# Down projection of a decoder step: the last norm in two token halves, the first of them inside the second pass

## What is computed

```python
def rmsnorm(x, g):
    xf = x.astype(jnp.float32)
    y = xf * lax.rsqrt(jnp.mean(xf * xf, axis=-1, keepdims=True) + EPS)
    return (y * g.astype(jnp.float32)).astype(x.dtype)
...
    f = (jax.nn.silu(h @ w_ff_gate) * (h @ w_ff_up)) @ w_ff_down
    x = x + ga2 * rmsnorm(f, g_post_ffn)
```

## Time and profile before

| | us |
|---|---|
| median of 3 runs | 2390.45 (2389.07 to 2390.79) |
| span of the profiled execution | 2391.5 |
| TensorE busy in the span | 2167.8 (91%) |
| VectorE, ScalarE, GpSimd busy | 880.6, 434.5, 501.2 |
| `stage_ffn_down`, first to last product | 276.1 |
| from the last product to the end | 49.8 |

### The profile page before, as it was taken

How to read it: one execution, slowest core, us unless ns; L and a number is a source line. 1 busy time by engine, 2 the same in 40 slices (tenths; PEclk the granted TensorE clock), 3 DMA queues, 4 the chain that set the end, 5 groups by cost and what they waited for, 6 DMA issues and landing times. The chain is left out here.

```text
span 2391.5 us, 31036 instructions
## 1 busy us (share of the span) xinstructions
PE 2167.8 (91%) x11898; PEld 1749.6 (73%) x11898; DVE 880.6 (37%) x1519; ACT 434.5 (18%) x896; POOL 501.2 (21%) x453
## 2 busy tenths in 40 slices
PE   3789999897778888999999998799999999999994
PEld 3678888676445565788888664688888888888883
DVE  1444122662345665522121116522222222534336
ACT  0241000331234555110000012311111000000001
POOL 2112210012211111521211113622223222001002
PEclk9899999895789999999999999899999999999997
DMA  9432112654410000111211210311111111122421
GB/s 240 120 95 75 44 36 57 184 130 132 116 49 1 2 1 1 36 45 27 53 26 44 90 51 3 108 35 53 35 52 36 36 53 35 49 97 84 152 79 73
DMA packets 238588, 157.35 MB, mean 66 GB/s; under 512 B 34502, under 2 KB 230632, under 8 KB 238417
## 3 DMA queue, kind: packets, MB, share of 16 engines
q1 hardware_dynamic: 224734, 138.33, 20.5%
q0 software_dynamic: 3600, 14.78, 1.8%
q10 hardware_dynamic: 10146, 2.80, 0.6%
HBM read 143.33 MB, written 16.71 MB: 67 GB/s over the span
## 5 line engine op out<-in xcount | busy, mean ns | idle before, releaser
L210 PE MATMUL ps<-hT,ring 128*128 128x264 f32 x2144 | 495.9, 389 | 18.7 <-DVEq L3025 14.8
L210 PE MATMUL ps<-big,ring 128*128 128x264 f32 (+1 forms) x2080 | 503.2, 400 | 4.5 <-DVEq L2863 4.5
L210 PEld LDWEIGHTS ps<-hT,ring 128*128 128x128 f32 x2144 | 410.2, 192 | 91.4 <-DVEq L3025 14.9
L210 PEld LDWEIGHTS ps<-big,ring 128*128 128x128 f32 x2080 | 396.0, 190 | 101.3 <-DVEq L2863 4.9
L3230 PE MATMUL ps<-big,ring 128*128 128x264 f32 x1056 | 240.7, 388 | 2.9 <-PEq L3417 2.9
L3230 PEld LDWEIGHTS ps<-big,ring 128*128 128x128 f32 x1056 | 201.7, 191 | 38.1 <-issue 3.2
L210 PE MATMUL ps<-big 128*128 128x264 f32 x608 | 138.5, 386 | 0.0
L210 PEld LDWEIGHTS ps<-big 128*128 128x128 f32 x608 | 115.4, 190 | 20.1 <-issue 0.4
L2610 DVE TENSOR_TENSOR big<-big,ps 128x528 f32<-128x528 f32 x70 | 49.3, 704 | 184.7 <-PE ps L210 177.2
L3080 POOL TENSOR_TENSOR ring<-ring 128x512 f32<-128x512 f32 x22 | 30.0, 1365 | 366.1 <-DMA ring<-in_w_ff_up 363.9
L975 DVE TENSOR_TENSOR big<-big,ps 128x528 f32<-128x528 f32 x63 | 44.2, 703 | 163.7 <-PE ps L210 163.3
(11 more groups left out here) (454 smaller groups left out, 2596.7 us busy)
## 6 DMA issues: line engine op xcount, KB each, us to landing
ring<-in_w_ada SPq DMA_DIRECT2D x44, 512.0 KB, 5.5
ring<-in_w_in SPq DMA_DIRECT2D x34, 512.0 KB, 5.1
ring<-in_w_ff_down SPq DMA_DIRECT2D x16, 1024.0 KB, 4.9
ring<-in_w_ff_gate SPq DMA_DIRECT2D x22, 512.0 KB, 4.0
ring<-in_w_ff_up SPq DMA_DIRECT2D x22, 512.0 KB, 5.2
ring<-in_w_ff_down SPq DMA_DIRECT2D x8, 768.0 KB, 4.2
x_kept<-big SPq DMA_DIRECT2D x8, 528.0 KB, 7.5
big<-x_kept SPq DMA_DIRECT2D x16, 264.0 KB, 6.2
```

The costliest lines, as they stand in the source:

```text
L210: ins = pe.matmul(out, w[:, k, :], rhs(k), start=first and k == 0, stop=last and k == nk - 1)
```

## The change

Line 3037 of `stage_ffn_up` writes the hidden values in token order, so pass 0 of the down projection holds tokens 0 to 527 whole and pass 1 tokens 528 to 1055. The rest is in `stage_ffn_down`:

- `tile`, the squares and the additions to `acc` work on whole token halves.
- At the start of steps 13 and 16 (c = 1 of pairs 4 and 5) TensorE sums 264 columns of the first half's `acc` into the free bank; at the end of these steps' queue of sums VectorE adds EPS and takes the reciprocal (`inverse`). Behind pair 4's squares ScalarE waits for both and takes one root. GpSimd then multiplies all eight tiles of the first half, ahead of adding the squares of pair 5. VectorE's eight `residual` steps stand two each behind the weight sums in steps 18, 19, 21 and 22.
- The squares of the last pair are no longer added by GpSimd: TensorE sums `acc` and the two squares into one bank for each 264 columns.
- ScalarE takes the two last roots between the copies of row tiles 1 and 2, and 2 and 3. Both must be done before the second half is scaled.
- The row tiles are twelve of 88 tokens: tiles 0 to 5 need the first half alone, 6 to 11 all of the second, sample tokens included. Three PSUM buffers of two banks and six row buffers serve them. The last tile is stored as 56 rows of `y_p` and 32 of `y_s`.

```diff
-                        f = to[:, bass.ds(it * 2 + hh, 1), :].rearrange("p o (n h t) -> p (o h) n t", h=2, n=2)
+                        f = to[:, bass.ds(it * 2 + hh, 1), :].rearrange("p o (h n t) -> p (o h) n t", h=2, n=2)
...
+YT = 88
+YN = T // YT
...
     def tile(s, unit, h):
-        return m.hT[:, unit, HALF * h + NH * s:HALF * h + NH * (s + 1)]
+        return m.hT[:, unit, HALF * s + NH * h:HALF * s + NH * (h + 1)]
...
         @block.gpsimd
-            for t in range(2 * N_SUM):
-                n = t // 2
-                a = both(m.acc[:, :], n // (N_SUM // 2))
+            for t in range(LATE):
+                if t == KD + 2:
+                    pool.wait_ge(rt_ok, 1)
+                    for k in range(KD):
+                        f = m.hT[:, k, 0:HALF]
+                        pool.tensor_tensor(f, f, rst[0], ALU.mult).then_inc(scaled, 1)
+                a = m.acc[:, halves[t // KD]]
...
         @block.tensor
+                if c == 1 and FIRST <= n < FIRST + 2:
+                    x = n - FIRST
+                    pe.wait_ge(pre, 1)
+                    pe.wait_ge(acc_ok, 1 + KD)
+                    pe.wait_ge(joined, 7 * (n - 1) + 6)
+                    pe.matmul(ps[:, bank(n, 7), 0:NH], ones, m.acc[:, NH * x:NH * (x + 1)], start=True,
+                              stop=True).then_inc(ss_mm, 1)
...
+                if c == 0 and FIRST < n <= FIRST + 2:
+                    pe.wait_ge(ss_out, n - FIRST)
...
+            pe.wait_ge(acc_ok, 1 + LATE)
+            pe.wait_ge(joined, 7 * (N_SUM - 2) + 6)
+            pe.wait_ge(copied, N_SUM)
+            for x in range(2):
+                pe.matmul(ps[:, x, 0:NH], ones, m.acc[:, HALF + NH * x:HALF + NH * (x + 1)], start=True, stop=False)
+            for t in range(2):
+                pe.wait_ge(sq_ok, LATE + t + 1)
+                for x in range(2):
+                    ins = pe.matmul(ps[:, x, 0:NH], ones, sq[t][:, NH * x:NH * (x + 1)], start=False, stop=t == 1)
...
         @block.scalar
+                if n == FIRST:
+                    act.wait_ge(r_ok, 2)
+                    act.activation(rst[0], rst[0], ACT.Sqrt).then_inc(rt_ok, 1)
+            for i in range(YN):
+                if i in (2, 3):
+                    x = i - 2
+                    r = rst[1][:, NH * x:NH * (x + 1)]
+                    act.wait_ge(r_ok, 3 + x)
+                    act.activation(r, r, ACT.Sqrt).then_inc(rt_ok, 1)
...
         @block.vector
+                if c == 1 and FIRST <= n < FIRST + 2:
+                    x = n - FIRST
+                    inverse(x, bank(n, 7), rst[0][:, NH * x:NH * (x + 1)])
+                if c < 2 and n >= FIRST + 2:
+                    if n == FIRST + 2 and c == 0:
+                        dve.wait_ge(x2_in, 16 * 2 * KD)
+                    for k in range(2):
+                        residual(4 * (n - FIRST - 2) + 2 * c + k)
```

More of the change, by code:

```diff
@@ L3146, in stage_ffn_down @@
             (m.ring[:, 2, 0:4, :], m.ring[:, 2, 4:8, :], block4(spare[:, 512:1024]))]
-    sq = [spare[:, 1024 + HALF * i:1024 + HALF * (i + 1)].rearrange("p (h t) -> p h t", h=2) for i in range(2)]
+    sq = [spare[:, 1024 + HALF * i:1024 + HALF * (i + 1)] for i in range(2)]
     ones = m.rest[:, 9 * NH:9 * NH + P]
-    rst = m.products[:, 0:T]
-    rows = [m.products[:, T + D * i:T + D * (i + 1)] for i in range(4)]
+    rst = [m.fore[:, KD + s, 0:HALF] for s in range(2)]
+    NR = 6
+    rows = [m.products[:, D * i:D * (i + 1)] for i in range(NR)]
     steps = [Down(m, i, sums[i % 2]) for i in range(len(STEPS))]
@@ L3195, in _ @@
                             sp.dma_start(x2(k, h), m.x2_kept[:, k, halves[h]]).then_inc(x2_in, 16)
-            for i in range(TT):
+            for i in range(YN):
                 rows_ready(sp, i)
[L3198 to L3203, removed]
+                n = min(YT, SEQ - YT * i)
+                sp.dma_start(O["y_p"][0, YT * i:YT * i + n, :], rows[i % NR][0:n, :]).then_inc(stored[i % NR], 16)
+                if n < YT:
+                    sp.dma_start(O["y_s"].rearrange("b s d -> (b s) d"), rows[i % NR][n:YT, :]).then_inc(
+                        stored[i % NR], 16)
+            for i in range(NR):
+                sp.wait_ge(stored[i], 16 * (len(range(i, YN, NR)) + (i == (YN - 1) % NR)))
         @block.gpsimd
@@ L3214, in _ @@
                 pool.tensor_tensor(a, a, sq[t % 2], ALU.add).then_inc(acc_ok, 1)
[L3216 to L3220, removed]
+            for lo, hi in late:
+                for k in range(1, KD, 2):
+                    pool.wait_ge(rt_ok, 3)
+                    f = m.hT[:, k, lo:hi]
+                    pool.tensor_tensor(f, f, rst[1][:, lo - HALF:hi - HALF], ALU.mult).then_inc(scaled, 1)
         @block.tensor
@@ L3255, in _ @@
                 one(6, q.s4, q.b22)
-            pe.wait_ge(pre, 1)
-            pe.wait_ge(acc_ok, 1 + 2 * N_SUM)
-            pe.wait_ge(joined, 7 * N_SUM)
[L3259 to L3267, removed]
+            pe.wait_ge(acc_ok, 1 + LATE)
[7 more added lines that the diff above has]
+                    ins = pe.matmul(ps[:, x, 0:NH], ones, sq[t][:, NH * x:NH * (x + 1)], start=False, stop=t == 1)
+                    if t:
+                        ins.then_inc(ss_mm, 1)
+            pe.wait_ge(joined, 7 * N_SUM)
+            for i in range(YN):
+                g = i // 3
+                pe.wait_ge(y_ok, KD if g < 2 else 2 * KD + 1)
+                if i >= 3:
+                    rows_ready(pe, i - 3)
                 for k in range(KD):
-                    ins = pe.transpose(ps[0:n, 2 * (i % 4) + k // 4, (k % 4) * P:(k % 4 + 1) * P],
-                                       m.hT[:, k, i * P:i * P + n], m.ident[:, :])
+                    ins = pe.transpose(ps[0:YT, 2 + 2 * (i % 3) + k // 4, (k % 4) * P:(k % 4 + 1) * P],
+                                       m.hT[:, k, i * YT:(i + 1) * YT], m.ident[:, :])
                 ins.then_inc(yT, 1)
@@ L3288, in _ @@
                     squares(n, x)
[L3289 to L3293, removed]
-                act.wait_ge(yT, i + 1)
[L3295 to L3299, removed]
+                if n == FIRST:
+                    act.wait_ge(r_ok, 2)
+                    act.activation(rst[0], rst[0], ACT.Sqrt).then_inc(rt_ok, 1)
+            for i in range(YN):
+                if i in (2, 3):
[3 more added lines that the diff above has]
+                    act.activation(r, r, ACT.Sqrt).then_inc(rt_ok, 1)
+                act.wait_ge(yT, i + 1)
+                if i >= NR:
+                    act.wait_ge(stored[i % NR], 16)
+                for c in range(2 if i < YN // 2 else 1):
+                    rows_out(i, c)
         @block.vector
@@ L3352, in join, with inverse, residual @@
                     add(p, p, 2)
+            def inverse(x, b, to):
+                dve.wait_ge(ss_mm, x + 1)
+                ins = dve.tensor_scalar(to, ps[:, b, 0:NH], EPS, None, ALU.add)
+                ins.then_inc(ss_out, 1)
+                dve.wait_ge(ss_out, x + 1)
+                dve.reciprocal(to, to).then_inc(r_ok, 1)
+            def residual(k):
+                dve.wait_ge(scaled, k + 1)
+                f = m.hT[:, k, 0:HALF]
+                dve.scalar_tensor_tensor(out=f, in0=f, scalar=m.modT[:, GA2 + k, 0:1], in1=x2(k, 0), op0=ALU.mult,
+                                         op1=ALU.add).then_inc(y_ok, 1)
             hidden(0)
@@ L3369, in _ @@
                     join(i, False)
[L3370 to L3386, removed]
+                n = i // 3
@@ new lines, in _ @@
+                if c == 1 and FIRST <= n < FIRST + 2:
[6 more added lines that the diff above has]
+                        residual(4 * (n - FIRST - 2) + 2 * c + k)
+            for x in range(2):
+                inverse(2 + x, x, rst[1][:, NH * x:NH * (x + 1)])
@@ new lines, in _ @@
+            for lo, hi in late:
+                for k in range(KD):
+                    f, r = m.hT[:, k, lo:hi], rst[1][:, lo - HALF:hi - HALF]
+                    dve.wait_ge(rt_ok, 3)
+                    if k % 2 == 0:
+                        chain(dve.tensor_tensor(f, f, r, ALU.mult))
+                    else:
+                        dve.wait_ge(scaled, KD + k // 2 + 1)
+                    dve.scalar_tensor_tensor(out=f, in0=f, scalar=m.modT[:, GA2 + k, 0:1],
+                                             in1=x2(k, 1)[:, lo - HALF:hi - HALF], op0=ALU.mult,
+                                             op1=ALU.add).then_inc(y_ok, 1)
```

35 lines of the change are left out of this document (18 added, 17 removed).

## The result

Over 20 runs of each, the changed kernel has a median of 2375.67 us and the kernel before 2389.08 us; the ratio is 0.9944, 95% interval 0.9922 to 0.9965, that is 13.4 us. The forecast was 13.7 us, 2376.8, range 2373.3 to 2381.5.

A forecast was written before the change was run, and what follows sets the result against it. TensorE alone bounds the down projection, then a 49.8 us relay of small steps, which the change targets. Terms +0.9 - 7.9 - 10.0 + 1.3 + 2.0 = -13.7 us give 2376.8 us, range 2373.3 to 2381.5.

The forecast's parts named there:

- Second pass: Second down-projection pass: two added ones-matmuls cost 0.9 us; the moved norm work on other engines adds 0.
- Way to the roots: Tail from last product to last root: 15.8 us falls to 7.9, gain 7.9; row copies late by 0.7.
- the low clock as a rival: Tail: TensorE falls to 1.2 GHz, right root at 12.0 instead of 7.9, total 2380.9 us; chance 8%.
- Scaling and residual: Late half: twelve VectorE instructions instead of 24, 22.2 us falls to 12.2, gain 10.0; first four at 1.7 each.
- full exclusion: Late scaling: GpSimd and two-SBUF-input VectorE instructions block each other wholly; twelve take 13.4 us, total 2378.0, within the forecast's range.
- To the first late store: End of residual to first late store: 2.85 us becomes 4.2, loss 1.3, as every late tile waits for sample steps.
- part 4: Late stores, first issue to end: 9.0 us becomes 11.0, loss 2.0.
- I take the upper: Late stores: an 88-row store costs 1.26 us like 128 rows, not 0.87 by bytes; end 11.0 rather than 10.2.
- the small store's landing: Late stores: landing of 3.8 against 2.9 taken to show that fewer rows do not go through faster.
- cited rule of the eleven engines: Late stores: 88 rows are split over 11 DMA engines, eight rows each, so a store costs the full 1.26 us.
- smaller rivals: Tail, same mechanism: stores by bytes 2376.0, GpSimd out of VectorE's way 2372.8, whole blocking 2378.0; 81% together with the forecast.
- rival of stalls in the second pass: Second pass: late GpSimd multiplications make TensorE wait; one stall cancels the gain, 4%, a second gives about 2405 us, 3%.

The follow-up runs named there:

- combined run: Changed kernel with 128-token row tiles, late half all on VectorE, both late roots before row tile 2's copies: tail 30.2 us, ratio 0.9906 to the kernel before.
- 80 + 8: Changed kernel with each 88-row store issued as 80 and 8 rows, the 56-row one as 48 and 8: first late store to end 11.1 us.
- 96: Changed kernel with row tiles of 96 tokens instead of 88: first late store to end 11.7 us, tail 34.0 us.
- halves: Kernel with 128-token row tiles, each store issued as two of 64 rows, partitions 0 to 63 and 64 to 127: first late store to end 11.3 us.
- even and odd rows: Kernel with 128-token row tiles, each store issued as two, its even and its odd rows: first late store to end 8.9 us.

## Why the prediction was right, and where not

**Second pass, right.** Cost 0.9, measured 0.9. VectorE's add and reciprocal took 2.26 (0.43 and 1.80) for 2.15, the root came 5 us early as argued, the multiplications ended before the next weight sums.

**Way to the roots, right**, 7.8 for 7.9: the copies ahead of the second root are what is late, but by 0.1 us and not by 0.7. The left sum was read at 2.8 for 2.45 and a reciprocal took 1.80 for 1.71, so the second inverse was ready at 7.2 for 6.85 (2327.47 + 1.80, counted from 2322.06). The combined run took the second root ahead of the copies and gained only 0.1. And the term did not say how much hung on the clock. The prediction carried the low clock as a rival at 8% with 4 us; the run with the squares on GpSimd shows that level, and the roots there came 2.4 us later than the additions alone explain (12.2 against 9.75). It was avoided by the edit itself, which leaves TensorE 0.3 us of idle time in place of 4.

**Scaling and residual, right in size.** 11.7 for 12.2. The interference of GpSimd was sized from before and is confirmed by taking it away. Not the first four instructions took 1.7 but the second to the fourth (3.21 for two, and 1.69); the first took 0.68. The full exclusion that the prediction took from the Trainium skill would have given 13.4: too much. In pairs, an instruction of each takes 1.6 to 1.7, less than the sum of 1.3 and 0.68.

**To the first late store, right**, 4.05 for 4.2: the wait for the sample steps (1.3) and the first tile at 0.50, as forecast; the second came 1.33 us later, not 1.65.

**Stores, too small.** The term that was mis-sized is part 4, in the step "I take the upper" of 0.87 and 1.26 us a store: 11.0, measured 12.4. The upper bound was none. It took 88 rows to cost at most what 128 cost, and took the rate of the earlier trace rows as the engines'. The reason given for it, the small store's landing of 3.8 us, does not bear it either: that store was issued with the engines full (2386.81, share 1.03), and with 128 rows in the changed kernel it landed in 3.0 like the large ones. The runs with 80 + 8, 96, halves and even and odd rows show that the partitions of the rows account for most of the loss: 252 to 283 GB/s in the changed kernel, so 352 KB (360,448 bytes) take 1.27 to 1.43 us each. The cited rule of the eleven engines describes the engines' share rightly (0.71) but is the smaller part of what binds: with 0.9 of the engines the rate was 262 to 275, and 1.3 of the 3.7 us came back.

The errors, -0.1, -0.5, -0.15 and +1.4, leave some 0.7 us: 12.9 by the profiles for 13.7. That is nearer than the store term alone would be, since three small errors ran against it, which is luck. One of the smaller rivals, 2372.8, was said to lie in the range and lies below its 2373.3; nothing hangs on it here. The rival of stalls in the second pass did not occur: no releaser but TensorE itself is in the chain there.

## What to carry to other kernels

A serial tail behind a long matmul pass is worth attacking by making a part of the output complete early, even if that needs another layout upstream: 12 us here for 0.9 us of TensorE time. When the pieces of the output are cut anew to fit such a split, check which partitions the store reads: 128 rows, or rows spread over all partitions, moved 400 GB/s, 88 or 64 neighbouring ones mostly 250 to 285. And when a short dependent chain stands between the matmuls and the next work of TensorE, the time of the chain is only part of its price: 4 us of idle time halved TensorE's clock for what followed.

## What the runs showed of the hardware

- A store's rate depends on the partitions it reads: even and odd rows of 128 in two transfers 404 GB/s, lower and upper half 268 to 285.
- Where stores fell behind, SP's issue itself grew: 0.33 us with whole tiles of 128 rows, up to 1.7 with 88 and 1.8 with 96.
- GpSimd and VectorE, both with two SBUF inputs, cost each other so much (VectorE's 0.68 becomes 1.7) that four multiplications of 496 columns handed to GpSimd made VectorE's part 0.9 us longer.
- After 4.0 us of waiting behind the dense products TensorE ran at a granted clock of 0.50; after 0.3 us it stayed at 1.00.
- In a stage that no edit touches (540 to 560 us) TensorE was granted 0.50 in nine profiles and 0.83 to 0.84 in three, and the down projection began at 2059.5 to 2065.8 us in the nine, at 2045.1 to 2048.1 in the three; the changed kernel was seen both ways. Why was not tried.
